# Shorter chains behind the stage norms, and TensorE multiplying constants at the norms and the spatial gate

## What is computed

```python
def rms_norm(x, w):
    y = x * rsqrt(mean(x * x, axis=-1) + EPS)
    return y * w

x = x + gate1 * (mix @ w_o)                             # stage "wo"
h2 = rms_norm(x, norm2_w) * (1 + scale2) + shift2       # norm "2"
up = h2 @ ffn_w_up                                      # 44 tiles "fa", "fv"
x = x + gate2 * ((a_path * v_path) @ ffn_w_down)        # stage "fd"
# second block
xn = rms_norm_2(h, norm1_g)                             # norm "3"
proj = xn @ w_in                                        # "cv0", "cg", "ca", "su", ...
y_a = spatial_gating(gelu(sg_u), gelu(sg_v), ...)       # 128x128 blocks, the spatial gate
h = h + merged @ w_out                                  # stage "w2"
ff = square(relu(rms_norm_2(h, norm2_g) @ w_ff1))       # norm "4", "up0".."up3"
h = h + ff @ w_ff2                                      # "do0".."do3"
ple_gate = sigmoid(rms_norm_2(h, norm3_g) @ w_ple_gate + b)   # norm "5", "pg"
h = h + ple_gate * (p @ w_ple)                          # "ple" is computed early, beside norm "2"
```

## Time and profile before

| | us |
|---|---|
| median of three runs | 2515.84 (2515.55 to 2520.0) |
| the profiled execution, its own time | 2516.51 |
| its span, first to last instruction | 2514.7 |
| mean granted TensorE clock | 0.965 of full |

### The profile page before, as it was taken

The page is one execution under the profiler, slowest core; times in us unless marked ns, Lnnn a source line. Parts: engine busy times, 40 slices in busy tenths (PEclk is TensorE's granted clock), DMA queues, the critical chain, the costliest instruction groups (busy, mean ns, idle before and its releaser), DMA issues.

```text
span 2514.7 us, 26819 instructions
## 1 busy us (share of the span) xinstructions
PE 2351.3 (94%) x10928; PEld 1879.2 (75%) x10928; DVE 1087.0 (43%) x1588; ACT 943.6 (38%) x1364; POOL 700.6 (28%) x415
## 2 busy tenths in 40 slices
PE   8898999999899999899999888999999999999996
PEld 3677888985577687688888676787777787888875
DVE  2566564446443323433321699413443243332333
ACT  2655343223442432533322332334552433332334
POOL 1142144002111244222232232311232353433332
PEclk9999999999999899999999898999999999999998
DMA  8222222221122132433333422232221332333331
GB/s 267 74 86 65 79 68 76 61 75 46 38 69 69 51 109 86 128 93 95 101 93 100 126 75 66 78 101 68 84 68 59 117 93 76 109 92 96 105 118 51
DMA packets 347982, 220.64 MB, mean 88 GB/s; under 512 B 18393, under 2 KB 327244, under 8 KB 347860
## 3 DMA queue, kind: packets, MB, share of 16 engines
q1 hardware_dynamic: 338462, 202.31, 27.6%
q10 hardware_dynamic: 9398, 16.62, 2.0%
HBM read 210.49 MB, written 8.41 MB: 87 GB/s over the span
## 4 chain that ended last, share of the span: by engine, by line
PE 76%; DVE 11%; ACT 7%; issue 3%; POOL 2%; DMA 2%; ACTq 0%; SPq 0%; DVEq 0%; POOLq 0%
PE ps L341 75%; DVE arena L367 4%; DVE arena L359 2%; ACT arena L356 2%; ACT whi L356 1%; POOL wlo L359 1%; PE ps L344 1%; DMA wraw<-in_w_in_dram 1%; ACT scr L356 1%; POOL arena L359 1%; DVE scr L367 1%; ACT L352 1%; DVE wlo L359 1%; DVE arena L364 1%; ACT L356 0%
## 5 line engine op out<-in xcount | busy, mean ns | idle before, releaser
L359 POOL TENSOR_TENSOR wlo<-wraw,whi 128x1024 fp32r<-128x1024 f32 (+1 forms) x163 | 391.3, 2400 | 1163.7 <-ACT whi L356 1163.7
L341 PE MATMUL ps<-hhi,whi 128*128 128x512 f32 x1664 | 454.0, 413 | 29.0 <-ACT whi L356 19.6
L356 ACT ACTIVATE whi<-wraw 128x1024 fp32r<-128x1024 f32 (+1 forms) x328 | 340.7, 1040 | 366.4 <-PE ps L341 295.1
L341 PE MATMUL ps<-hhi,wlo 128*128 128x512 f32 x1664 | 422.3, 393 | 4.6 <-POOL wlo L359 4.6
L341 PE MATMUL ps<-hlo,whi 128*128 128x512 f32 x1664 | 421.8, 392 | 1.2 <-POOL hlo L359 1.2
L341 PEld LDWEIGHTS ps<-hhi,whi 128*128 128x128 f32 x1664 | 319.1, 196 | 114.1 <-issue 39.7
L341 PE MATMUL ps<-arena 128*128 128x128 f32 (+6 forms) x2304 | 346.3, 305 | 44.5 <-ACT arena L356 26.8
L359 DVE TENSOR_TENSOR wlo<-wraw,whi 128x1024 fp32r<-128x1024 f32 (+2 forms) x165 | 223.3, 1353 | 374.0 <-ACT whi L356 373.8
L341 PEld LDWEIGHTS ps<-hhi,wlo 128*128 128x128 f32 x1664 | 315.2, 189 | 72.2 <-POOL wlo L359 6.2
L341 PEld LDWEIGHTS ps<-hlo,whi 128*128 128x128 f32 x1664 | 316.3, 190 | 69.6 <-POOL hlo L359 1.6
L341 PEld LDWEIGHTS ps<-arena 128*128 128x128 f32 (+1 forms) x2304 | 292.5, 201 | 77.5 <-issue 33.9
(11 more groups left out here) (190 smaller groups left out, 2554.8 us busy)
## 6 DMA issues: line engine op xcount, KB each, us to landing
wraw<-in_w_in_dram SPq DMA_DIRECT2D x99, 512.0 KB, 3.9
wraw<-in_w_ff_dram SPq DMA_DIRECT2D x64, 512.0 KB, 4.0
wraw<-in_ffn_w_up_dram SPq DMA_DIRECT2D x44, 512.0 KB, 3.8
wraw<-in_w_ada_dram SPq DMA_DIRECT2D x32, 512.0 KB, 3.9
wraw<-in_w_gate_dram SPq DMA_DIRECT2D x32, 512.0 KB, 3.6
arena<-in_w_ada_dram SPq DMA_DIRECT2D x8, 1024.0 KB, 11.6
wraw<-in_ffn_w_down_dram SPq DMA_DIRECT2D x16, 512.0 KB, 3.6
wraw<-in_w_branch_dram SPq DMA_DIRECT2D x16, 512.0 KB, 3.4
```

The lines of the kernel that those rows point to most:

```text
L341: return pe.e.matmul(o, l, r, start=start, stop=stop)
L356: return ac.e.activation(o, i, f, bias=bias, scale=scale, **kw)
L359: return q.e.tensor_tensor(o, a, b, op)
```

## The change

Four edits. **The sum of squares:** POOL no longer adds tile 7's square in the four stage norms; TensorE's sum becomes two accumulating matmuls, one of `SQT` after POOL's add for tile 6, one of tile 7's square (`SCR[1]`) right after ScalarE wrote it. **The table:** the Ln and Exp table is loaded at the first tile of the stage. **Constants:** a new `fill` multiplies `ones` by the first 512 columns of the constants n times into a bank that nobody reads: 5 times ahead of each norm's sum, 7 times behind it, and 13 times ahead of the spatial products, 61 in all. **Norm 2:** VectorE multiplies tile k by the modulation column and by the root in one instruction; ScalarE adds the shift and writes the high part in one pass; VectorE alone makes the low part, of tile k - 1 after it has made tile k. POOL has no part in it.

```diff
+        def load_log_exp():
+            if not log_exp[0]:
+                ac.e.preload_act_table_set("natural_log_exp_and_others")
+            log_exp[0] = True
...
-        H2 = Split("h2", HP, even_po)
+        H2 = Split("h2", HP, lambda k: "ve")
...
-            def rsum(self, sem, label, tile, dve_point):
-                bk = PA.take(sem, label)
-                pe.wait_ge(*PA.free(sem, label))
-                pe.wait_ge(*at(*dve_point))
-                mm(bk[:, :], ones, tile, True, True).then_inc(*inc(sem, label))
-                PA.put((sem, label), "nr_act", "ln", label)
+            def fill(self, label, n):
+
+                bk = PA.take("fill", label)
+                pe.wait_ge(*PA.free("fill", label))
+                for _ in range(n):
+                    t = mm(bk[:, :], ones, CST[:, 0:512], True, True)
+                t.then_inc(*inc("fill_mm", label))
+                PA.put(("fill", label), "fill_mm", label)
+
+            def rsum(self, label, stage):
+
+                self.fill((label, 0), 5)
+                bk = PA.take("nr_mm", label)
+                pe.wait_ge(*PA.free("nr_mm", label))
+                pe.wait_ge(*at("sq_po", stage, 6))
+                mm(bk[:, :], ones, SQT, True, False)
+                pe.wait_ge(*at("sq_act", stage, 7))
+                mm(bk[:, :], ones, SCR[1], False, True).then_inc(*inc("nr_mm", label))
+                PA.put(("nr_mm", label), "nr_act", "ln", label)
+                self.fill((label, 1), 7)
...
                 t.then_inc(*inc("sp_mm", "w"))
                 PA.put(("sw",), "sp_act", "w")
                 yield
+                self.fill(("s", 0), 13)
                 for g in range(4):
...
             def ev_wo(self, m, bk):
+                if m == 0:
+                    load_log_exp()
...
                     ac.wait_ge(*at("n2_ve", k))
                     ac.wait_ge(*at("mod_ve", 3, 0))
-                    ac.wait_ge(*at("mod_ve", 4, 1))
-                    act(A[:, 22 + k, :], A[:, 22 + k, :], ACT.Identity, bias=modcol(3, k), scale=modcol(4, k)).then_inc(
-                        *inc("n2_act", k))
-                    ac.wait_ge(*at("n2_act", k))
-                    self.high(H2, k, A[:, 22 + k, :])
+                    act(H2.hi[k], A[:, 22 + k, :], ACT.Identity, bias=modcol(3, k)).then_inc(*inc("x_hi", "h2", k))
...
             def norm2(self, extra):
                 ve.wait_ge(*at("nr_act", "ri", "2"))
                 ve.wait_ge(*at("mix_po", 7))
-                for k in range(8):
-                    tt(ve, A[:, 22 + k, :], XR[k], SCR[2], ALU.mult).then_inc(*inc("n2_ve", k))
-                    self.low(H2, k, A[:, 22 + k, :])
+                ve.wait_ge(*at("mod_ve", 4, 1))
+                for k in range(9):
+                    if k < 8:
+                        stt(A[:, 22 + k, :], XR[k], modcol(4, k), SCR[2], ALU.mult, ALU.mult).then_inc(*inc("n2_ve", k))
+                    if k:
+                        ve.wait_ge(*at(*H2.high_point(k - 1)))
+                        stt(H2.lo[k - 1], A[:, 21 + k, :], modcol(3, k - 1), H2.hi[k - 1].bitcast(F32), ALU.add,
+                            ALU.subtract).then_inc(*inc("x_lo_ve", "h2", k - 1))
...
             def add_square(self, stage, m, tmp):
-                if m:
+                if m and (m < 7 or stage == "pg"):
...
-            def norm2(self, extra):
-                for k in range(8):
-                    self.low(H2, k, A[:, 22 + k, :])
-                    if k % 2:
-                        next(extra, None)
+            norm2 = Plan.norm2
```

More of the change, by code:

```diff
@@ L350, in act @@
             if f in (ACT.Ln, ACT.Exp):
-                if not log_exp[0]:
-                    ac.e.preload_act_table_set("natural_log_exp_and_others")
-                log_exp[0] = True
+                load_log_exp()
             elif f not in (ACT.Copy, ACT.Identity, ACT.Square, ACT.Relu):
@@ L1443, in ple @@
                 yield from self.linear("ple", self.nothing)
-            def rsum(self, sem, label, tile, dve_point):
-                bk = PA.take(sem, label)
-                pe.wait_ge(*PA.free(sem, label))
-                pe.wait_ge(*at(*dve_point))
-                mm(bk[:, :], ones, tile, True, True).then_inc(*inc(sem, label))
-                PA.put((sem, label), "nr_act", "ln", label)
+            def fill(self, label, n):
[15 more added lines that the diff above has]
+                self.fill((label, 1), 7)
             def norm2(self, extra):
-                self.rsum("nr_mm", "2", SQT, ("sq_po", "wo", 7))
+                self.rsum("2", "wo")
                 for k in range(8):
@@ L1458, in norm3 @@
             def norm3(self):
-                self.rsum("nr_mm", "3", SQT, ("sq_po", "fd", 7))
+                self.rsum("3", "fd")
             def conv(self):
@@ L1598, in ff2_start @@
             def ff2_start(self):
-                self.rsum("nr_mm", "4", SQT, ("sq_po", "w2", 7))
+                self.rsum("4", "w2")
             def norm5(self):
-                self.rsum("nr_mm", "5", SQT, ("sq_po", "do", 7))
+                self.rsum("5", "do")
             def turn(self, m):
```

## The result

| | before | after |
|---|---|---|
| median, us | 2516.44 (2515.55 to 2520.0, 4 runs) | 2528.81 (2526.99 to 2530.25, 4 runs) |
| profiled execution, its own time | 2516.51 | 2530.25 |
| its span | 2514.7 | 2528.4 |
| mean granted TensorE clock | 0.965 | 0.972 |

The ratio is 1.0046, with a 95% interval of 1.0029 to 1.0064; the medians differ by 12.4 us, and the changed kernel is the slower one. The forecast was 2532 in a range of 2526 to 2538.

A forecast was written before the change was run, and what follows sets the result against it. TensorE, busy for 94% of the span, was taken as the bound; 3.8 (norm 2) + 0.7 (norm 3) + 0 (spatial gate) + 5.8 + 5.7 (norms 4, 5) = 16.0 us on 2515.84 gave 2532, range 2526 to 2538.

The forecast's parts named there:

- The price, 0.86 us per constant matmul: Each added f32 constant matmul takes TensorE 0.86 us at full clock, low end 0.227, high end 1.72.
- The two statements weighed there: Skill texts on constants' price: about 216 ns per 512-column matmul, no type named; four passes for true FP32.
- the other case: Rival: a constant matmul costs only 0.227 us, so the kernel is 10.5 us faster, 2505; chance 0.05.
- Norms 4 and 5: Ahead of `up0` and `pg`: fourteen f32 matmuls, TensorE never waits, next layers 5.8 and 5.7 us later.
- Spatial gate, 0: Thirteen constants start the products 2.4 us late; a later wait, shorter by 1, covers it: cost 0, else 1.
- Norm 2, +3.8: Ahead of the feed-forward: Ln 3.5 us later, ScalarE newly waits for `ple`, TensorE 3.8 us later; bounds 0 to 6.
- Norm 3, +0.7: Ahead of the second block: five constants and the two-part sum put Ln 0.7 us later; bounds 0 to 1.5.
- The rest, 0: No other place adds to the sum; moved table loads cost 0, at worst 1.3 us once.
- the sum of 16.0: Whole kernel: norms 2, 3, 4, 5 and spatial gate add 3.8 + 0.7 + 5.8 + 5.7 + 0 us.
- Cheap and half-priced constants: Two rivals: 0.227 us per constant gives 2505, chance 0.05; one 0.43 record each gives about 2514, chance 0.04.
- constants at the lower clock: Rival: 1.72 us each at one or two norms, or bank still held, 10 us more, 2542; chance 0.04.
- Partly absorbed: Rival: last-stage ScalarE waits or norm 2's zero low end absorb about 6 of 16 us, 2526; chance 0.07.

The follow-up runs named there:

- Experiment 3: The changed kernel with its 61 f32 constant matmuls replaced by fp32r ones of 40 partitions, same number and places: 2508.88 us, ratio 0.9963 to the kernel before.
- experiment 2: The changed kernel without the seven constants behind the sums of norms 4 and 5: 2517.04 us, ratio 1.0008 to the kernel before.
- experiment 5: The changed kernel with only the 13 constants at the spatial gate, none at the norms: 2500.02 us, ratio 0.9943 to the kernel before.
- experiment 1: The changed kernel without its 61 constant matmuls: 2499.91 us, ratio 0.9935 to the kernel before.
- experiment 8: The kernel before with only the new division of norm 2 (ScalarE one pass, VectorE all low parts): 2513.47 us, ratio 0.9992.
- experiment 7: The kernel before with only the two-part sum and early table load, old norm 2, no constants: 2503.45 us, ratio 0.9949.
- experiment 4: The kernel before with the 61 constants added at the same places, old sums and old norm 2: 2526.6 us, ratio 1.0044.
- experiment 6: The changed kernel with only three constants behind norm 3's sum and six ahead of `fu0`: 2497.61 us, ratio 0.9939 to the kernel before.

## Why the prediction was right

**The price, 0.86 us per constant matmul: right.** The records are 0.43 apart at all five places, and taking fourteen away saved 11.8 us where 14 x 0.86 is 12.0. The two statements weighed there come out as the trace of before had said. The 216 ns of the Trainium skill (TensorE: Matmul & The Clock Gate, section "Back-to-back issue gap"), given there for a single matmul, does not hold for f32 operands: 0.86 us here. The Trainium skill (FP8 and Floating Point Precision, section "TensorE Precision Notes") has four passes for a true FP32 product; the trace agrees in size, 3.8 times an fp32r matmul, and shows two records for it, not four. Experiment 3 is the other case made real: fp32r constants cost some 0.26 us, and 20 us vanish.

**Norms 4 and 5: right.** Forecast 5.8 and 5.7, measured 5.8 and 5.8. No gap of 3.54 is left, the clock is full, and the sevens cover nothing, as experiment 2 shows alone.

**Spatial gate, 0: right, with one sign wrong.** Against VectorE's memset the products start 2.0 us later than before (2.4 behind it where it was 0.4), for 2.4 forecast, and experiment 5 shows that all thirteen are free. But the wait behind them was to be shorter by 1 and stayed, 4.96 for 4.95: it begins when a matmul on a tile of ScalarE has run and ends with ScalarE's next; only the short wait ahead of that matmul became shorter, 0.51 for 0.78.

**Norm 2, +3.8: mis-sized, +4.9.** Its path was close: Ln came 3.4 later (forecast 3.5), ScalarE waits for `ple` inside its loop, and the second unit's low part lets TensorE go 3.3 later (1032.24 - 1006.46 for 22.46 before). What I left out is the clock behind it. TensorE idles 2.76 and 0.62 just ahead of that point, and the window after shows 0.50 over 4.7 us: from there to `fa` tile 1 it takes 12.05 (37.83 - 25.78) instead of 10.44 (32.90 - 22.46), 1.6 more. The new norm 2 brings most of it by itself: it takes 11.0 to 12.1 there without constants (experiments 1, 5, 8), the old one 10.4 (before, experiment 7) and 11.4 with constants (experiment 4). Twelve constants earlier in the norm did nothing for that, and experiment 6 shows that six of them in the right wait do.

**Norm 3, +0.7: mis-sized, -0.9.** Ln came 0.68 later from the end of `fd`, as forecast. But I let everything behind `cv0` move with it. Before, the wait of 2.70 was followed by eight matmuls at the lower clock; after, the wait of 1.92 was not, 1.5 us less. VectorE, whose convolution carries the stretch from there, shows 0.9 of it: in the trace of before it waits 0.88 us for TensorE at 1448.64, and in those of the kernel after and of experiment 2 it doesn't. The wait of 1.92 is shorter partly for another reason: ScalarE's issue of the load of `sg_ln_g` took 2.25 us in the trace of before and 1.34 in this one, in code that was not touched. It takes 1.33 in seven of the experiments and 2.49 in the other, so that 0.9 is chance. Together they bring the memset to 1.1 us earlier than before, counted from the end of `fd`. Experiment 4, with the old chain, has -1.0 in this stretch as well, but otherwise made up: its memset comes 0.4 later, and the gain is behind it. So -0.9 is within what traces of one code differ by here, and how it divides stays open.

**The rest, 0: the start was 1.5 shorter by chance.** Code that nothing touched differs by more between traces here: over all ten the start ends between 1005.6 and 1009.6, and the long stretch up to the end of `w2` takes 484.6 to 490.7. From the sum of 16.0 to the profiled 13.7: norm 2 +1.1, norm 3 -1.6, the start -1.5, the rest -0.3. The median differs by 12.4, since the profiled execution was the slowest of the four after and at the middle of those before.

**The rivals.** Cheap and half-priced constants, constants at the lower clock: refuted by the records. "Partly absorbed" gave 2526, which is as near to 2528.8 as the forecast of 2532 is, by luck. What it named, the lower end of zero at norm 2 and cover in the last stage, did not happen.

**What I had too low without noticing** is the worth of the chains. I expected about 10 us of experiment 1, before it ran, and it gave 16. Norm 3's stretch gained 5 to 7 where I had 2.6. The convolution behind it is VectorE's: the first normalised tile comes 2.7 us sooner, the memset 3.5 sooner in all four of experiments 1, 5, 6 and 7, and what is gained beyond that hangs in part on the low parts shown in experiment 5. That VectorE's earlier start is what carries the 3.5 through is my reading of these times; no run held it fixed.

## What to carry over

Filling a wait of TensorE with idle matmuls is free only for as long as TensorE would wait anyway. Price the filler by its operand type from a row of the trace, multiply, and set it against the gap after the chain has been shortened, since both eat the same gap. A filler behind a point from which useful matmuls could start is pure delay. And the clock it protects was worth something here only where TensorE bound the next stretch (`fu0`: 1.1 to 1.8 us for six fillers), not where it waited for its operands (norm 3, the spatial gate: nothing).

## What was not expected of the hardware

A gap of 1.20 us ahead of the second half of the sum left the granted clock at 1.00 at norms 4 and 5 (experiment 1); one of 3.54 at the same places was followed by 0.57 and 0.63 over 4 us. Shortening the wait gave back the clock that the constants were to hold.

In experiment 1, ScalarE's norm 2 loop is held once by one of its own stores. From its timeline:

```profile
1017.14 1.24 ACTq L1997 DMA_DIRECT2D pls_dram<-scr  x1
...
1023.10 0.60 ACT L359 ACTIVATE scr<-ps 128x512 f32<-128x512 f32 x1 [1.91 <-DMA pls_dram<-scr]
```

The store took about 6 us to land and the issue of it 1.24, where the other seven of the same shape take 0.33 to 0.35. The wait of 1.91 is for the scratch tile that the store reads and the next eviction overwrites. In the trace of experiment 5, the same code at norm 2, that wait is 0.95 and the issue 0.33, and norm 2 is 28.9 us there instead of 31.4; the store is one part of that difference, not shown to be all of it. So two traces of one code can differ by more at a place than an edit there is worth.
